# Two blocks, mixers of kind 1: the gates' products gathered in one place, the gelu's square and one rounding moved

## The reference

```
proj = h @ w_in        # lru_x 512, lru_g 512, sb_q/k/v 256 each, fx_q/k/v 256 each, fx_f 4
u = causal_depthwise_conv(lru_x, 4 taps) + b
r = sigmoid(u @ w_r + b_r); i = sigmoid(u @ w_i + b_i)        # 8 blocks of 64 x 64 each
log_a = -8 r softplus(-lam); a = exp(log_a)
y_lru = scan(a, sqrt(1 - a^2) * i * u) * gelu(lru_g)
y_sb  = stick_breaking_attention(sb_q, sb_k, sb_v)
y_fox = forgetting_attention(rms(fx_q), rms(fx_k), fx_v, log_sigmoid(fx_f + b))
out = concat(rms(y_lru), rms(y_sb), rms(y_fox)) * g @ w_out
```

## Time and profile before

| | |
|---|---|
| median of the runs | 1555.13 us |
| the profiled execution | 1553.34 us |
| its span, first to last instruction | 1551.5 us |
| TensorE busy | 1531.4 us, 99% |
| DVE busy | 1294.4 us, 83% |
| ACT busy | 911.6 us, 59% |
| POOL busy | 282.0 us, 18% |
| TensorE's granted clock, mean | 0.999 |

### The profile page before, as it was taken

One profiled execution on the slowest core, in us unless ns is written; L12 is line 12 of the kernel. 1 busy time (PEld: TensorE's weight loads), 2 busy tenths in 40 slices (PEclk: granted clock), 3 DMA queues, 4 the chain that ended last, 5 costly groups with the idle time before them and its releaser, 6 DMA issues.

```text
span 1551.5 us, 32204 instructions
## 1 busy us (share of the span) xinstructions
PE 1531.4 (99%) x13130; PEld 1512.1 (97%) x13130; DVE 1294.4 (83%) x1943; ACT 911.6 (59%) x1584; POOL 282.0 (18%) x288
## 2 busy tenths in 40 slices
PE   6999999999999999999999999999999999999998
PEld 6999999999999999999999999999999999999998
DVE  7998898997898888888998889889888889885553
ACT  6555468765555545459765455677555466765453
POOL 4322000112210222000113242101222201021100
PEclk9999999999999999999999999999999999999999
DMA  9999974479987899864579998445999963567761
GB/s 366 363 375 335 316 254 163 164 251 324 321 319 265 300 312 324 300 231 164 177 251 332 314 335 286 150 137 164 321 329 332 332 233 123 167 207 239 239 209 42
DMA packets 110612, 401.99 MB, mean 259 GB/s; under 512 B 12450, under 2 KB 12706, under 8 KB 110336
## 3 DMA queue, kind: packets, MB, share of 16 engines
q1 hardware_dynamic: 109136, 395.34, 73.2%
q0 software_dynamic: 1328, 4.58, 0.9%
HBM read 398.83 MB, written 1.05 MB: 258 GB/s over the span
## 4 chain that ended last, share of the span: by engine, by line
PE 88%; DVE 5%; ACT 4%; DMA 1%; issue 1%; DVEq 0%; SPq 0%; ACTq 0%
PE PS L626 87%; DVE WL L1909 2%; ACT WH L1373 1%; DMA ring<-in_up 1%; DVE SCR L1909 1%; DVE SCR L1912 1%; DVE SCR L2293 1%; DVE SMALL L2292 0%; ACT SCR L1701 0%; DVE ring L1935 0%; DMA ring<-in_ada 0%; PE PS L1215 0%; PE PS L827 0%; DVE SMALL L2332 0%; ACT HH L1405 0%
## 5 line engine op out<-in xcount | busy, mean ns | idle before, releaser
L1909 DVE TENSOR_TENSOR WL<-ring,WH 128x1024 fp32r<-128x1024 f32 (+1 forms) x502 | 603.5, 1236 | 151.9 <-ACT WH L1373 151.4
L626 PE MATMUL PS<-HH,WH 128*128 128x256 f32 (+2 forms) x2600 | 617.6, 279 | 1.9 <-DVE WL L1909 1.2
L626 PE MATMUL PS<-HL,WH 128*128 128x256 f32 (+1 forms) x2592 | 602.1, 277 | 0.0
L1373 ACT ACTIVATE WH<-ring 128x1024 fp32r<-128x1024 f32 (+1 forms) x502 | 507.0, 1050 | 44.2 <-PE PS L626 36.0
L626 PEld LDWEIGHTS PS<-HH,WH 128*128 128x128 f32 (+1 forms) x2600 | 488.2, 188 | 3.8 <-issue 2.6
L626 PEld LDWEIGHTS PS<-HL,WH 128*128 128x128 f32 x2592 | 481.1, 188 | 0.5
L626 PE MATMUL PS<-HH,WL 128*128 128x256 f32 (+1 forms) x2592 | 372.0, 277 | 0.4
L1935 DVE CUSTOM_DVE_ANT_0 ring<-ring,CB,VC 128x1024 f32<-128x1024 f32 x240 | 331.3, 1397 | 3.2 <-DMA ring<-in_ada 3.2
L626 PEld LDWEIGHTS PS<-HH,WL 128*128 128x128 f32 x2592 | 332.1, 188 | 1.3 <-DVE WL L1909 1.1
L626 PE MATMUL PS<-AH,WH 128*128 128x256 f32 x1056 | 292.4, 277 | 0.0
L626 PE MATMUL PS<-AH,WL 128*128 128x256 f32 x1056 | 292.1, 277 | 0.2 <-DVE WL L1909 0.2
(11 more groups left out here) (257 smaller groups left out, 1535.0 us busy)
## 6 DMA issues: line engine op xcount, KB each, us to landing
ring<-in_up SPq DMA_DIRECT2D x176, 512.0 KB, 5.7
ring<-in_ada SPq DMA_DIRECT2D x144, 512.0 KB, 6.1
ring<-in_ffn SPq DMA_DIRECT2D x132, 512.0 KB, 4.9
ring<-in_mod SPq DMA_DIRECT2D x96, 512.0 KB, 6.0
ring<-in_down SPq DMA_DIRECT2D x88, 512.0 KB, 5.8
ring<-in_win SPq DMA_DIRECT2D x64, 512.0 KB, 5.5
ring<-in_wout SPq DMA_DIRECT2D x32, 512.0 KB, 4.4
ring<-in_winv SPq DMA_DIRECT2D x8, 512.0 KB, 4.2
```

The source lines that it names most:

```text
L626: return e.matmul(out, lhsT, rhs, start=start, stop=stop, skip_group_check=skip)
L1373: e.activation(half_of(i)[0], slot_of(("half", i, 0))[:, 0:w], ACT.Copy).then_inc(s_hi, 1)
L1909: return e.tensor_tensor(out, a, b, op)
```

## The change

On TensorE, `columns` of unit 3 gets no products in between any more, and all four gates and all the forget products go between the halves of unit 4. On ACT, the rounding of half 5 goes ahead of the first `shifted`, and the projection of unit 3 and the square go ahead of the first two sigmoids; all four gates' sigmoids then follow each other. No instruction is added or removed, and DVE's, POOL's and SP's queues are as they were.

```diff
@@ TensorE, mixer1
                 columns(n, 2, 0, 0)
-                columns(n, 3, 1, 0, lambda: (gate(0), gate(1), forget(range(4))))
-                columns(n, 4, 0, 3, lambda: (gate(2), gate(3), forget(range(4, KD))))
+                columns(n, 3, 1, 0)
+                columns(n, 4, 0, 3, lambda: (gate(0), gate(1), gate(2), gate(3), forget(range(KD))))
                 columns(n, 5, 1, 4)
@@ ACT, mixer1
                 normalised(n)
+                hi_half(2 * u0 + 5)
                 shifted(n, 0, LX[:, 0:2, 3:259])
-                hi_half(2 * u0 + 5)
                 hi_half(2 * u0 + 6)
                 shifted(n, 1, LX[:, 2:4, 3:259])
                 hi_half(2 * u0 + 7)
                 projected(2, LG[:, 0:2, :], 0)
                 hi(u0 + 4)
+                projected(3, LG[:, 2:4, :], 1)
+                e.wait_ge(s_proj, p0 + 4)
+                e.activation(GT, LG, ACT.Square).then_inc(s_gelusq, 1)
                 gate_out(0)
                 gate_out(1)
-                projected(3, LG[:, 2:4, :], 1)
                 gate_out(2)
                 gate_out(3)
-                e.wait_ge(s_proj, p0 + 4)
-                e.activation(GT, LG, ACT.Square).then_inc(s_gelusq, 1)
                 hi(u0 + 5)
```

## The result

The changed kernel takes 1558.58 us (median of 18 runs, 1556.14 to 1560.98) against 1554.96 for the kernel before (18 runs, 1553.96 to 1556.57); the ratio is 1.0025, 95% interval 1.0019 to 1.0032, or 3.6 us. The forecast was +1.8 us: the sign and the wait were right, and nearly half of the loss was something that I had given a chance of 2%. Of all the runs reported here one, of the kernel with half 8's rests first, took 3121.30 us, twice the time of its ten others, and is left out of that kernel's ratio.

What follows compares the result with a forecast made beforehand. TensorE, busy 99% of the span, was the bound. Per mixer 1.69 us late less 0.33 and 0.5 left about 0.9; two mixers gave +1.8 us, 1556.9 us; own range 1555.2 to 1558.2, 8 in 10 1553.8 to 1559.4.

Steps and rivals of the forecast that it cites:

- TensorE's own work unchanged: TensorE: the same 16 gate instructions and 16 forget products are issued, half moved from unit 3 to 4; no time taken.
- The moved rounding brings DVE 0.80 us: ACT rounds half 5 before line 1506, so DVE's stream up to half 8's rests comes 0.80 us earlier.
- the second rival: Line 1506, now later, holds DVE at the first convolution, so the rounding brings nothing: +3.4 us, 1558.5 us; chance 9%.
- The new wait of 2.0 us: TensorE stalls 2.0 us before half 8's rests, because DVE has the convolutions of chunks 2 and 3 queued first.
- the 1.69 us at unit 5: After the stall and the gathered gates, TensorE ends half 9 and reaches unit 5 1.69 us late, per mixer.
- Old waits that give back 0.83 us: TensorE's waits at half 13's rests (0.33 us) and the fox scores (0.5 us) go, in each mixer.
- Break even: Rival: stall as predicted, but 0.9 us more per mixer comes back at later TensorE waits: 1555.1 us; chance 14%.
- The table load behind the square: ACT's table load (1.28 us) runs behind the gelu's square, before the gate block begins at 233.22, without waiting for gates.
- All sigmoids behind the block: ACT: all eight sigmoids come behind the gathered gates and forget products; the last ends at about 237.6 us.
- by the row the stall costs only itself: TensorE's clock: a 5.0 us wait for x showed granted clock 1.00, so the 2 us stall would cause no fall.
- the third rival: Clock falls behind each new stall, halving TensorE's speed: 8.1 us more per mixer, +18 us in all, 1573 us; chance 2%.
- Slower by over 0.2%: Whole kernel's time above 1558.2 us; given 0.15.

Runs made afterwards that it cites:

- The kernel with the wait filled: Changed kernel plus 17 products nobody reads on TensorE before its wait for half 8's rests, in each mixer of kind 1: 1556.63 us, ratio 1.0010 against the kernel before.
- the half-filled kernel: Changed kernel plus 8 products nobody reads, in place of 17, before TensorE's wait for half 8's rests: 1556.62 us, ratio 1.0012 against the kernel before.

## Why the prediction was right, and where it was not

- TensorE's own work unchanged: right, 1531.4 and 1532.1 us busy with 13130 instructions each.
- The moved rounding brings DVE 0.80 us: right, 0.80 by the profile (0.8 us in all as a change of its own, inside its interval). Line 1506 behind it held nothing up, so the second rival fell.
- The new wait of 2.0 us, its release by DVE's line 1909, and the 1.69 us at unit 5: right (1.82 us of idle, 2.0 by starts; 1.6 us). The cover was lost as described: with the rests ahead of two convolutions the wait is gone.
- Old waits that give back 0.83 us: right in kind. The fox scores do not wait, and 1.59 - 0.88 = 0.71 us came back. That 0.88 us per mixer remain, where I took 0.9, is in part luck: 0.1 us less lateness and 0.1 us less given back cancel. The kernel with the wait filled has that sum alone: 1.9 us measured, 1.8 forecast. Break even fell with it.
- The table load behind the square: right. All sigmoids behind the block: they start inside it, at 234.53, and end at 237.96 - 0.26 = 237.70, where I had 237.6.
- **The step that failed is "by the row the stall costs only itself".** I read from the earlier trace rows that 5 us of idle time left the clock at 1.00, and took the third rival down to 2%. Amid dense products an idle time of 1.9 us brought the granted clock to 0.50 behind half of the waits seen. The Trainium skill's warning ("TensorE: Matmul & The Clock Gate", "HAM oscillation") came true in kind, though the idle gaps that it speaks of are longer than these; the measurement decides against my reading. The rival's price was wrong too, 8.1 us per mixer: in the change's profile a fall cost 1.97. On average over the runs it cost 3.6 - 1.9 = 1.7 us, less than one fall in an execution.
- The row itself did not say what I took from it. Right behind the wait for x, 16 products of line 1325 take 3.68 us in the kernel before. In the profile of the change without the rounding they take 3.67 us there and only 1.97 us in the next group of 16, of the same shape (the first line is the kernel before's):
```profile
10.58 3.68 PE L1325 MATMUL PS<-CN,SCR 128*128 128x128 f32 x16 [4.96 <-DMA SCR<-in_x]
...
11.23 3.67 PE L1325 MATMUL PS<-CN,SCR 128*128 128x128 f32 x16 [5.25 <-DMA SCR<-in_x]
16.44 1.97 PE L1325 MATMUL PS<-CN,SCR 128*128 128x128 f32 x16 [1.54 <-ACT SCR L1852]
```
  The granted clock is given as 1.00 for both groups, so a 1.00 in these first microseconds is no evidence of full pace: the products behind the wait that I held up as harmless took 1.9 times as long (3.67 / 1.97) as the group that followed.
- The lower end of the forecast's own range, 1555.2, doesn't follow from its terms, which give 1556.9 - 0.8 - 0.5 = 1555.6. Nothing else hangs on it.
- "Slower by over 0.2%" had 0.15 and is what came (0.25%, interval 0.19 to 0.32), by this term alone; without it, as with the wait filled, the change is about 0.12% slower.

## What to carry to other kernels

Before work is moved out from between two steps of the busy engine, ask what the other engines did under its cover: here the gates hid two convolutions ahead of a subtraction in DVE's queue, and moving that subtraction turned 3.6 us slower into 2.9 us faster. A wait of TensorE amid dense work had two prices here, its length less what later waits give back, and a possible fall of the clock; if the wait can't go, products in it can take away the second, as 17 useless ones did here, and 8 in another kernel. An edit made of three parts is to be taken apart: two of the three were worth 2.6 us, and the one that stands first in the change's name cost 6.2 us on top of them (3.6 + 2.6).

## What the chip showed that I had not expected

The clock fell behind waits of 1.8 to 1.9 us, 4 of 8, and behind neither of the two of 0.99 us in the half-filled kernel; each kernel was profiled in one execution. The spread of the runs points the same way: 4.8 us in the changed kernel, 1.2 us with the wait filled, 2.2 us with it half filled, 2.6 us in the kernel before.

A fall does not need this wait. In two of the twelve profiled executions, those of the forget products in the wait and of the gathering in the first mixer, the granted clock was also 0.50 near the start, at 22 to 24 us. TensorE had idled there for 1.53 us and then for 2.30 in the one and 2.48 in the other; in the change without the rounding it idled for 1.54 and 2.26 and the clock stayed at 1.00. The first of the two:
```profile
22.00:23.00 1.00, 0.62 (x2) 0.00 (x0) 1.00 (x1) 0.97 (x2) 1.00 (x1) 0.50 1.03 410
```
